# Expert gate and up weights: two contiguous halves of a slot in place of pieces of 256 floats

## The reference

```
x = xn.reshape(B * T, D)                                     # D = 1024
_, idx = lax.top_k(scores + router_bias, TOP_K)              # 8 of 64 experts a token
hid = silu(einsum('nd,edf->nef', x, exp_w_gate)) * einsum('nd,edf->nef', x, exp_w_up)     # f = 256
routed = einsum('nef,efd->nd', hid * gates[..., None], exp_w_down)
shared = (silu(x @ shared_w_gate) * (x @ shared_w_up)) @ shared_w_down
```

## Time and profile before

| | |
|---|---|
| three timed runs | 984.48, 993.21 (median), 999.41 us |
| profiled execution | span 998.1 us from first to last instruction; its time outside the span is not given |
| TensorE matmul busy | 798.7 us (80%), mean granted clock 0.884 of full |
| VectorE, ScalarE, GpSimd busy | 393.9, 235.7, 306.1 us |
| DMA | 277.75 MB in 192,230 packets, 154,931 of them from 512 B to under 2 KB |
| q1 (SP's loads) | 165,654 packets, 250.88 MB, busy 72.3% of 16 engines' span |
| q0 (GpSimd's transfers) | 21,216 packets, 22.57 MB, 10.2% |
| experts | from 258.6 us to about 950 us |

### The profile page before, as it was taken

One profiled execution on the slowest core, in us unless ns is written; L12 is line 12 of the kernel. 1 busy time (PEld: TensorE's weight loads), 2 busy tenths in 40 slices (PEclk: granted clock), 3 DMA queues, 4 the chain that ended last, 5 costly groups with the idle time before them and its releaser, 6 DMA issues.

```text
span 998.1 us, 16529 instructions
## 1 busy us (share of the span) xinstructions
PE 798.7 (80%) x5564; PEld 449.7 (45%) x5565; DVE 393.9 (39%) x825; ACT 235.7 (24%) x405; POOL 306.1 (31%) x285
## 2 busy tenths in 40 slices
PE   1979999999888799876796888888788788887910
PEld 1657555445444355443443444444444344443500
DVE  2235183656144643233342343334334334444306
ACT  2112543023132222122121221222122122222202
POOL 0120000021133444344334343433334434344323
PEclk8879999999897889878888889887888988988965
DMA  9977846345689999989998999899899989999234
GB/s 273 398 244 240 304 164 231 117 149 212 226 251 362 367 318 334 324 251 348 311 316 287 315 316 327 252 349 310 281 340 321 360 285 334 358 331 353 68 58 145
DMA packets 192230, 277.75 MB, mean 278 GB/s; under 512 B 20355, under 2 KB 154931, under 8 KB 183548
## 3 DMA queue, kind: packets, MB, share of 16 engines
q1 hardware_dynamic: 165654, 250.88, 72.3%
q0 software_dynamic: 21216, 22.57, 10.2%
q10 hardware_dynamic: 5254, 2.76, 1.1%
HBM read 270.14 MB, written 25.89 MB: 297 GB/s over the span
## 4 chain that ended last, share of the span: by engine, by line
PE 54%; DMA 26%; issue 10%; DVE 6%; POOL 1%; POOLq 1%; ACT 1%; SPq 1%; DVEq 0%
DMA et<-xn_rows,idx 16%; PE bank L1049 15%; PE bank L1085 12%; DMA acc_rows<-et,idx 5%; PE bank L770 4%; PE bank L778 3%; PE bank L1032 3%; PE bank L913 3%; PE bank L797 2%; DMA gu<-in_ada_w 2%; PE bank L755 2%; DMA small<-halfc 2%; PE bank L1009 1%; PE bank L1136 1%; PE bank L781 1%
## 5 line engine op out<-in xcount | busy, mean ns | idle before, releaser
L1049 PE MATMUL bank<-gu,et 128*64 128x256 f32 x2496 | 295.9, 394 | 33.3 <-issue 31.0
L1049 PEld LDWEIGHTS bank<-gu,et 128*64 128x64 f32 x2496 | 185.6, 144 | 168.2 <-issue 91.4
L1085 PE MATMUL bank<-dn,et 128*64 128x512 f32 x624 | 183.5, 726 | 2.3 <-DVE et L1534 1.2
L449 POOL DMA_INDIRECT acc_rows<-et,idx x64 | 105.6, 1649 | 226.1 <-DVE et L1541 164.1
L430 POOL DMA_INDIRECT et<-xn_rows,idx x64 | 80.8, 1263 | 193.9 <-DVE idx L1516 133.7
L1534 DVE COPY et<-bank 128x256 f32<-128x256 f32 x64 | 27.1, 424 | 222.8 <-PE bank L1066 218.6
L690 ACT ACTIVATE et<-bank 64x512 f32<-64x512 f32 x64 | 37.8, 590 | 265.9 <-PE bank L1049 263.1
L1032 PE MATMUL bank<-ident,et 128*128 128x128 f32 x256 | 50.0, 328 | 62.3 <-DMA et<-xn_rows,idx 35.6
L1085 PEld LDWEIGHTS bank<-dn,et 128*64 128x64 f32 x624 | 46.6, 163 | 88.7 <-issue 88.7
L1520 DVE COPY et<-bank 128x512 f32<-128x512 f32 x64 | 44.3, 692 | 103.5 <-PE bank L1032 99.9
L1541 DVE TENSOR_SCALAR et<-bank,pick_out 128x512 f32<-128x512 f32 x64 | 48.1, 751 | 81.4 <-PE bank L1085 76.5
(11 more groups left out here) (269 smaller groups left out, 684.0 us busy)
## 6 DMA issues: line engine op xcount, KB each, us to landing
gu<-in_exp_w_gate SPq DMA_DIRECT2D x64, 1024.0 KB
gu<-in_exp_w_up SPq DMA_DIRECT2D x64, 1024.0 KB
dn<-in_exp_w_down SPq DMA_DIRECT2D x64, 1024.0 KB
gu<-in_ada_w SPq DMA_DIRECT2D x12, 2048.0 KB, 13.9
gu<-in_w_in SPq DMA_DIRECT2D x4, 2048.0 KB, 19.5
gu<-in_w_out SPq DMA_DIRECT2D x2, 2048.0 KB, 13.1
acc_rows<-dn SPq DMA_DIRECT2D x2, 1280.0 KB, 16.2
small<-halfc POOLq DMA_DIRECT2D x100, 0.0 KB
```

Of the source, the lines that this page charges most:

```text
L449: pool.indirect_dma_start(acc_rows[0], bass.IndirectOffsetOnAxis(ap=idx[:, u, 0:1], axis=0), yo[:, u % 2, 0, :], None, bounds_check=2 * T ...
L1049: mm = pe.matmul(bank[u % 2][64 * c:64 * c + 64, b * FE:(b + 1) * FE], xt[:, b, k % 4, k // 4, :], w[:, k, c * FE:(c + 1) * FE], start=(k ...
L1085: mm = pe.matmul(bank[5 + b][64 * c:64 * c + 64, :], hT[:, b, j, :], dn[:, dslot(u), j * D + c * HALF:j * D + (c + 1) * HALF], start=(j == ...
```

## The change

The slot is now seen as two halves. Gate fills floats 0 to 2047 of a partition, up floats 2048 to 4095, each as one contiguous run of 8 KB on both sides of the transfer. The matmuls read block `k` of gate or up in its half: 256 contiguous floats as before, at another address. The shared expert's loads change in the same way, and its product for the first two token tiles, which took one run of 512 floats, now takes two runs of 256 floats in one matmul with 512 columns. The mixer's weights keep their form. No instruction is added, removed or put in another place on any engine; only line numbers move.

```
-        eg = io["exp_w_gate"][0].rearrange("e (p k) f -> e p k f", k=KT)
-        eu = io["exp_w_up"][0].rearrange("e (p k) f -> e p k f", k=KT)
+        eg = io["exp_w_gate"][0].rearrange("e (p k) f -> e p (k f)", k=KT)
+        eu = io["exp_w_up"][0].rearrange("e (p k) f -> e p (k f)", k=KT)
...
+        def halves(slot):
+            return gu[slot][:, :, :].rearrange("p k n -> p (k n)").rearrange("p (c m) -> p c m", c=2)
+
+        def pair(slot):
+            return halves(slot).rearrange("p c (k f) -> p c k f", k=KT)
...
-                sync.dma_start(gu[SH_SLOT][:, :, c * FE:(c + 1) * FE],
-                               io[name][0].rearrange("(p k) f -> p k f", k=KT)).then_inc(ld_shared_gu, 16)
+                sync.dma_start(halves(SH_SLOT)[:, c, :],
+                               io[name][0].rearrange("(p k) f -> p (k f)", k=KT)).then_inc(ld_shared_gu, 16)
...
-                sync.dma_start(gu[gslot(u)][:, :, 0:FE], eg[e]).then_inc(ld_gu[gslot(u)], 16)
-                sync.dma_start(gu[gslot(u)][:, :, FE:2 * FE], eu[e]).then_inc(ld_gu[gslot(u)], 16)
+                sync.dma_start(halves(gslot(u))[:, 0, :], eg[e]).then_inc(ld_gu[gslot(u)], 16)
+                sync.dma_start(halves(gslot(u))[:, 1, :], eu[e]).then_inc(ld_gu[gslot(u)], 16)
...
-            def shared_gu(t):
-                tile_product(bank[4 + t], t, gu[SH_SLOT], 2 * FE).then_inc(s["sh_ready"], 1)
+            def shared_product(t, ks):
+                t0, n = TILES[t]
+                w = pair(SH_SLOT)
+                for k in ks:
+                    if t < 2:
+                        mm = pe.matmul(bank[4 + t][:, :].rearrange("p (c f) -> p c f", c=2), xT[:, k, t0:t0 + n], w[:, :, k, :],
+                                       start=(k == 0), stop=(k == KT - 1))
+                    else:
+                        for c in range(2):
+                            mm = pe.matmul(bank[4 + t][64 * c:64 * c + 64, 0:FE], xT[:, k, t0:t0 + n], w[:, c, k, :],
+                                           start=(k == 0), stop=(k == KT - 1))
+                return mm
...
-                w = gu[gslot(u)]
+                w = pair(gslot(u))
...
-                                           w[:, k, c * FE:(c + 1) * FE], start=(k == 0), stop=(k == KT - 1))
+                                           w[:, c, k, :], start=(k == 0), stop=(k == KT - 1))
```

More of the change, by code:

```diff
@@ L962, in _ @@
             pe.wait_ge(ld_shared_gu, 32)
-            tile_product(bank[4], 0, gu[SH_SLOT], 2 * FE, range(4))
+            shared_product(0, range(4))
             turn("z", "xn_ready", 1)
-            tile_product(bank[4], 0, gu[SH_SLOT], 2 * FE, range(4, KT)).then_inc(s["sh_ready"], 1)
+            shared_product(0, range(4, KT)).then_inc(s["sh_ready"], 1)
             pe.wait_ge(s["tp_evac"], TP["z11"] + 1)
@@ L981, in _ @@
             spread_gf(3)
-            tile_product(bank[5], 1, gu[SH_SLOT], 2 * FE, range(4))
+            shared_product(1, range(4))
             pe.wait_ge(s["mask_done"], 1)
@@ L995, in _ @@
             mm.then_inc(s["tp_ready"], 1)
-            tile_product(bank[5], 1, gu[SH_SLOT], 2 * FE, range(4, KT)).then_inc(s["sh_ready"], 1)
+            shared_product(1, range(4, KT)).then_inc(s["sh_ready"], 1)
             def pick(r, i, u):
@@ L1152, in rounds @@
                     pe.wait_ge(s["gf_in"], 6)
-                    shared_gu(2)
+                    shared_product(2, range(KT)).then_inc(s["sh_ready"], 1)
                 pick(r, 0, 1)
```

## The result

The changed kernel took 1014.54 us (median of four runs, 1010.76 to 1021.33); the kernel before, run beside it, 994.6. That is 20 us more where the forecast had 6. It lies in the range of 968 to 1024, but nearer to the rival "slower" (1021) than to the likeliest case (999).

The account below looks back on a forecast made before the run. It took PE's waits for token gathers on q0, beside q1's stream, as the bound, not the weights. Gathers gave +3.2 us for 25, late ones and the clock +3: +6 us, so 999 us, range 968 to 1024.

Parts of the forecast that it names:

- the rival "slower": q0 beside q1's 8 KB runs: every gather served like the third write, 1.1 us a wait, +28 us, 1021; chance 0.21.
- Transfers 0, SP's issues 0: Gate and up loads: 64 us less transfer, all beside other work; SP only waits longer for slots: 0 each.
- Matmuls 0: Experts' matmuls read the same 256 contiguous floats: 0; shared product's two-run reads, possibly 2.7 us, taken as 0.
- The turns of the loop: PE ahead of L1049: five stalls, read as its code being fetched, should stay at 31 us.
- the first kind: Ten of 21 gather pieces, 7.9 us or more, taken as already served beside 8 KB: gain 0.5 us each.
- The second kind: Eleven of 21 gather pieces, 7.7 us or less, would come to 7.8 us: +0.7 us each.
- gathers that just made it before now may not: Gathers PE did not wait for may now be late; with longer idle time, one or two more give +3 us.
- The bound for it, +1.1 us: Gather's service on q0: pure 1 KB to pure 8 KB costs at least +1.1 us, from the three writes.
- a gather's first wait: Wait on q0 for the first packet goes by q1's bytes, 3.7 us to 3.2: -0.5 us for each gather.
- the 1033 us: Rival: q0 gets its turn only after 17 of q1's descriptors, +1.6 us on 25 waits, +40 us; chance 0.05.
- The clock: Down matmuls after longer PE idle run at the 1.2 GHz level; one or two more such cases: +3 us.
- the faster one: Rival: freed engine time empties q1 before the gather's turn, -0.9 us a wait, -22 us, 971; chance 0.12.

Follow-up runs that it names:

- b_dn1k: Kernel before, with the down matrices also in 1 KB pieces, gate and up staying at 1 KB: 972.49 us, ratio 0.9782 to the kernel before.
- no_all: Changed kernel with gate, up and down loads cut to 32 bytes a partition from the ninth expert on: 869.51 us, ratio 0.8724 to the kernel before.
- p2k: Changed kernel with gate and up in 2 KB pieces instead of 8 KB runs: 999.31 us, ratio 1.0036 to the kernel before.
- p4k: Changed kernel with gate and up in 4 KB pieces instead of 8 KB runs: 1003.49 us, ratio 1.0102 to the kernel before.

## Why the prediction was right and wrong

*What bounds the kernel: right.* Tokens, not weights. b_dn1k and no_all show it from both sides: more work for the DMA engines and less time, then no weights and hardly a wait.

*Transfers 0, SP's issues 0: right.* SP's waits took the gain up (above). One thing differed without a cost: SP's longest issue of an up matrix took 5.86 us before (first row, of the kernel before) and takes 0.84 us now (second row, of the changed one).
```profile
589.08 5.86 SPq L308 DMA_DIRECT2D gu<-in_exp_w_up  x1
```
```profile
830.25 0.84 SPq L314 DMA_DIRECT2D gu<-in_exp_w_up  x1
```

*Matmuls 0: right.* The experts' take 395 ns against 394. The two reads in one matmul of the shared product cost nothing: between 230 and 255 us such a matmul takes 605 ns in both kernels (first the kernel before, then the changed one), far from 2 x 382.
```profile
L778 PE MATMUL bank<-gu,xT 128*128 128x512 f32 x16 | 7.4, 605 | 0.0
```
```profile
L957 PE MATMUL bank<-gu,xT 128*128 128x512 f32 x16 | 7.4, 605 | 0.0
```
Over the whole run the profile counts 32 such instructions, not sixteen, so the case that the prediction priced at 2.7 us and set to 0 would have been 5.4.

*The turns of the loop: right.* 31.9 us. The experiments add what holds them up: 30.4 us without the down loads, but 18.0 without gate and up and 17.8 without any. I read this as the code's transfers standing behind q1's gate and up, by bytes; 8 KB packets instead of 1 KB made no difference (31.9 against 31.0).

*The gathers: the right mechanism, but the sum was too small, and this is the step that was off.* "I take the first kind as served beside 8 KB now: they keep their service and gain 0.5 us. The second kind joins them: 8.3 - 0.5 = 7.8." The two kinds were there. In the 2.5 us up to the landing of each of the 21 pieces of before, q1's packets and megabytes give 85% of the bytes in 8 KB packets for the ten long pieces and 26% for the eleven others. (With n packets and B bytes, (B - 1024 n)/7168 of them are of 8 KB. For the pieces issued at 490.23 and 893.51 us:
```profile
q1 hardware_dynamic: 147, 0.84, 84.2%
```
```profile
q1 hardware_dynamic: 783, 0.92, 103.5%
```
96 of 147, and 17 of 783.) But with all packets at 8 KB the pieces did not draw together at 7.8: twelve of 23 last 7.9 us or more, with a mean of 8.82, and the others have 7.52. The mean rose by 0.56 us where the sum had 2.7/21 = 0.13.

Compared expert by expert, the prices for one gather were about right. Eight of the ten long pieces stand in the new chain too and are 0.58 us shorter on the mean (forecast: 0.5); ten of the eleven others do, and are 1.02 us longer (forecast: 0.7, "rather too much"). Part of this would come by itself, since the ten were picked as the longest of one execution: in p2k and p4k they are 0.63 and 0.69 us shorter as well, and the others 0.50 and 0.53 longer. What the sum had too small is its other term, "gathers that just made it before now may not". Five pieces of the new chain have no counterpart in the old one, and they take 8.10 to 9.92 us, mean 9.18. PE's waits say the same: for the ten experts of the long kind they fell from 41.0 to 29.9 us, for the eleven others they rose from 30.1 to 37.3, and for all further gathers from 7.3 to 16.6. That last term is +9.3 us; the prediction had one or two more stretches at the low clock for it, +3 in all. The largest single one is the gather of the 36th expert (first the kernel before, then the changed one):
```profile
649.86 0.65 PE L1028 MATMUL bank<-ident,et 128*128 128x128 f32 x4 [1.57 <-issue]
```
```profile
656.78 1.11 PE L1044 MATMUL bank<-ident,et 128*128 128x128 f32 x4 [5.40 <-issue]
```
All this is the profiled pair, 10.6 us apart. How the 20 us between the medians divide no profile shows. 25 waits at 0.56 us are +14, and with 0.5 of it again for the clock +21, which would fit; but it is a sum made afterwards, and in the profiled pair the waits grew by 5.3 us only.

*The bound for it, +1.1 us: wrong in its making.* It compared a 512 KB write beside 1 KB with a 256 KB write beside 8 KB. Like with like, the price is 1.5 to 2.4 us for the large one and at most 0.4 for the small, less than the small one's own scatter; the mean of the chain's pieces rose by 0.56. That the rival "slower" gave 1021, close to what came, is partly luck: it had 1.1 us a wait and no clock.

That a gather's first wait goes by bytes and falls with the rate (-0.5 us) was not tested by a run of its own; the 0.58 us of the eight pieces above agrees with it, but so do those of p2k and p4k. The Trainium skill, "DMA: Bandwidth & Descriptors", section "Queues, rings and completion order", has an engine take about 9 to 17 descriptors from one queue before it turns to the next. What follows from that rule in direction, that larger descriptors make another queue wait longer, is what the table of sizes shows, against my objection; the 1033 us that I drew from it for 17 of them are not: 1014.5. Whether one descriptor or several go at a turn no run here tells.

*The clock: term in the right direction, too small.* +3 us was set for one or two more cold stretches. The profile shows +3.6 us of busy time, beside the +9.3 of waits above; how much it is between the medians is not shown.

*"Gathers draw together at 7.8; over 8.3 is the slower rival, under 7 the faster":* 8.20, at the rival's door, and the time fell there too. *"The waits sum to about 82":* 83.8 in the profiled execution, the shortest of four.

## What to carry to other kernels

Where a bulk stream has slack and a small transfer on another queue is what the compute engine waits for, the bulk stream's packets want to be small, not large: 8 KB against 1 or 2 KB cost 2 to 5% here, while the DMA engines looked emptier. Look which load stands in the queue beside the critical transfer: here the packets of the down matrix, a third of the bytes, counted as much as those of gate and up or more. When waits are added up, ask also which transfers have just made it so far and will be waited for now. And price every microsecond of waiting on TensorE with what the clock takes on top, here 0.5 us.

## What the runs showed of the hardware

A DMA share of 1 was no bound here: at 1.06 (b_dn1k, from 300 to 850 us) the kernel was faster than at 0.87.
```profile
300.00:850.00 550.00, 465.77 (x3260) 254.91 (x3260) 217.42 (x476) 128.94 (x209) 228.29 (x209) 0.89 1.06 331
```
q1 alone, in 8 KB runs of gate and up between 221.3 and 224.9 us of the changed kernel, moved 1.50 MB, 417 GB/s, where the same stretch of before moved 1.25 MB in 1 KB pieces:
```profile
q1 hardware_dynamic: 215, 1.50, 103.1%
```
Packets of 2 KB cost q1 little time against 8 KB: its share is 64.8% of 1008.7 us with all expert matrices at 8 KB, 70.6% of 975.6 at 2 KB and 78.4% of 970.5 at 1 KB, which is 654, 689 and 761 us.
